# Prompt attention turned round: values stationary in two column tiles, and one product to turn the result back

## The chip, the core and the metric

The kernel runs on one core of one Trainium2 chip. The metric is the device time of one execution in microseconds (us), the median of the runs that were timed.

## The reference, cut to what matters

One layer of a hybrid encoder for a prompt of 1024 tokens and for 8 short sample sequences. The change touches one part, the attention of the prompt ("FoX", 16 heads of width 64, in float32):

```
s = (q_b . k) * 64**-0.5 + cq[q] - ck[key]     # q_b: a block of 128 queries, ck: cumulative log-forget gate
s = -inf where key > query                     # so block b sees the b + 1 key blocks up to its own
y = softmax(s) @ v                             # v: keys x 64
```

Around it stand the projection of the tokens (`z = RMSNorm(x) @ w_in`), an mLSTM over the same tokens, the attention of the samples, a merge, an expert layer (top 16 of 16384 single-neuron experts in each of 8 heads, whose rows are gathered from HBM), and a last gate. All outputs of all parts are returned.

## The kernel before

The whole layer is one program of stages with a barrier between them. Each engine has its own list of instructions, written out in order by hand, and counts semaphores to wait for the others. An engine never passes an instruction that waits, so the order of its list is part of the design.

The prompt attention stands in two stages, both built by `stage_attend`. The **small stage** takes query blocks 0 and 1 (`NB` = 2, so 32 steps of one head and one block, with 1 or 2 key blocks each; about 427 to 551 us of the span). The **large stage** takes blocks 2 to 7 (`NB` = 6, 96 steps, 3 to 8 key blocks, 5.5 in the mean; about 1855 to 2586 us). In both, the mLSTM of the same tokens rides along: 32 slots for each chunk of 128 tokens, two in each step (`ml.*_slot`, slot numbers k). In the large stage expert work rides as well (`ex.*_unit`): for each of 44 groups VectorE makes 4 dot products (L2394), ScalarE applies a Gelu to them (L2437), and VectorE weighs and adds 4 rows (L2401, L2410). There is about one Gelu in two steps, at a changing place in the step.

A step s of the attention (class `FoxPrompt`) is this chain:

1. `pe_scores` (L547, L549): TensorE makes the scores of 128 queries against up to 1024 keys in PSUM, and adds the mask. In the large stage there is one buffer for scores, so it waits until step s-1 was exponentiated.
2. `dve_max` (L581): VectorE takes the row maximum.
3. `act_exp` (L608): ScalarE makes the probabilities, and their sum.
4. `pe_turn` (L555): TensorE transposes them, a block of 128 keys at a time.
5. `act_probs` (L616): ScalarE copies the transposed blocks to `probT`.
6. `pe_mix` (L569): TensorE mixes. For each key block the 128x128 `probT` is the stationary operand and 64 columns of v are the moving one; the blocks add up in the bank `fy`.
7. `dve_y` (L588, L593): VectorE scales by the inverse sum into `y`.

The lists run this chain with an offset. TensorE's iteration s has: scores of s; transposes of the next head's q and k (`pe_head`, L531); an mLSTM slot; the turn of s-1; an mLSTM slot; the mix of s-1. ScalarE's: copies of the next head; a slot (half 0); the probability copies of s-1; the exponential of s; Gelus; a slot (half 1); Gelus. VectorE's: the maximum of s; the scaling of s-2; slots and expert units. The mix of s-1 waits for the scaling of s-2 (`y_ready`), which comes behind the maximum of s.

A float32 matmul stands in the trace as two records, each with its own weight load; a transpose is one record.

Of the kernel before, what the change touches and what calls it, by code (L numbers as in the profile page):

```python
# [17 lines left out]
ALU = mybir.AluOpType  # L18
# [3 lines left out]
P = 128  # L22
# [7 lines left out]
H_F, DF = 16, 64  # L30
# [392 lines left out]
class FoxPrompt:  # L423

    def __init__(self, nc, K, st, z, T, b0, b1):
# [9 lines left out]
        self.nmax, self.total, self.inv = (st.sb(n, [P, 2]) for n in ("fnmax", "ftotal", "finv"))  # L435
        self.y = st.sb("fy", [P, 2, NB, P])
        self.s_ps, self.y_ps = st.ps("fs", [P, 1024]), st.ps("fy", [P, 512])
        self.t_bank = [st.ps(f"ft{n}", [P, 512]) for n in range(2)]
        (self.ones_set, self.t_full, self.t_free, self.scored, self.maxed, self.expd, self.inverted, self.mixed,
         self.y_ready) = st.sems("f_ones_set f_t_full f_t_free f_scored f_maxed f_expd f_inverted f_mixed f_y_ready")  # L440
        self.qk_in, self.ck_in, self.v_in, self.y_out = (
# [93 lines left out]
    def pe_scores(self, pe, s):  # L535
        hd, b = divmod(s, self.NB)
        if s == 0:
            pe.wait_ge(self.ones_set, 1)
        if b == 0:
            pe.wait_ge(self.t_free, self.use["head", hd, len(self.groups) - 1] + 1)  # L540
            pe.wait_ge(self.ck_in[hd % 2], (hd // 2 + 1) * 16)
        if s >= self.SBUFS:
            pe.wait_ge(self.expd, s - self.SBUFS + 1)
        out, n = self.score_bank(s), self.blocks(s) * P
        for c in range(0, n, 512):
            w = min(512, n - c)
            pe.matmul(out[:, c:c + w], self.qT[:, hd % 2, b * P:(b + 1) * P], self.kT[:, hd % 2, c:c + w],  # L547
                      start=True, stop=(c + w != n))
        pe.matmul(out[:, n - P:n], self.K["ident"][:], self.K["mask"][:], start=False, stop=True).then_inc(self.scored, 1)  # L549
# [9 lines left out]
    def pe_mix(self, pe, s, r):  # L559
# [8 lines left out]
        for c in range(4 * r, min(4 * r + 4, n)):  # L568
            mm = pe.matmul(self.y_ps[:, 0:DF], self.probT[:, c * P:(c + 1) * P],  # L569
                           self.v[:, i % 2, c, e * DF:(e + 1) * DF], start=(c == 0), stop=(c == n - 1))  # L570
        if r == self.rounds(s) - 1:
            mm.then_inc(self.mixed, 1)

    def dve_first(self, dve):
        dve.memset(self.qT[DF:DF + 1, :, :], 1.0).then_inc(self.ones_set, 1)

# [7 lines left out]
    def dve_y(self, dve, s):  # L584
# [4 lines left out]
        dve.wait_ge(self.inverted, s + 1)  # L589
        dve.wait_ge(self.mixed, s + 1)  # L590
        if i >= 2:
            dve.wait_ge(self.y_out[i % 2], i // 2 * 16)
        dve.tensor_scalar(self.y[:, i % 2, b, e * DF:(e + 1) * DF], self.y_ps[:, 0:DF], self.inv[:, s % 2:s % 2 + 1],  # L593
                          None, ALU.mult).then_inc(self.y_ready, 1)
# [459 lines left out]
def stage_attend(nc, K, z, bias, cache_lf, gates, ck_last, C, m, T, b0, b1, ex=None, g0=0, g1=0):  # L1054

    with Stage(nc, f"att{b0}") as st:
# [37 lines left out]
        def _(pe):  # L1094
# [3 lines left out]
            ga.pe_scores(pe)  # L1098
            for s in range(STEPS + 1):
                if s < STEPS:  # L1100
                    fx.pe_scores(pe, s)
                    for hd, g in fx.heads_at(s):
                        fx.pe_head(pe, hd, g)
                    ml.pe_slot(pe, *slot(s, 0))
                if s >= 1:
                    for r in range(fx.rounds(s - 1)):
                        fx.pe_turn(pe, s - 1, r)
                if s < STEPS:
                    ml.pe_slot(pe, *slot(s, 1))
                if s >= 1:  # L1110
                    for r in range(fx.rounds(s - 1)):
                        fx.pe_mix(pe, s - 1, r)

        @block.scalar
        def _(act):
# [3 lines left out]
            ga.act_probs(act)  # L1119
            for s in range(STEPS + 1):  # L1120
                if s < STEPS:
                    for hd, g in fx.heads_at(s):
                        fx.act_head(act, hd, g)
                    ml.act_slot(act, *slot(s, 0))
                if s >= 1:
                    for r in range(fx.rounds(s - 1)):
                        fx.act_probs(act, s - 1, r)
# [1832 lines left out]
def trunk_kernel(nc, A, O):  # L2960
# [15 lines left out]
    with ExitStack() as ctx:  # L2976
        def sb(name, shape, dt=F32):
            return ctx.enter_context(nc.sbuf_tensor(name, shape, dt))

        K = {n: sb(n, [P, P]) for n in ("ident", "ones", "negones", "mask", "maskT", "tri", "bmask", "bmaskT", "btri",  # L2980
                                        "last", "blast")}
        K["pick"], K["inblock"] = sb("pick", [P, NSEQ]), sb("inblock", [P, NSEQ])
        K["headsel"] = sb("headsel", [H_F, 2, 8, DSEQ])
        K["masknew"] = sb("masknew", [P, DSEQ])
# [13 lines left out]
        with ExitStack() as front:  # L2998
# [4 lines left out]
            aT_later = later.enter_context(nc.sbuf_tensor("aT_later", [P, KD, (NT - FIRST) * P], F32, side="right"))  # L3003

            with nc.sbuf_tensor("aT", [P, KD, FIRST * P], F32) as aT:
                stage_front(nc, K, A["x"], A["norm_mix"], aT, aT_later, A["w_in"], z)
            stage_attend(nc, K, z, A["gate_bias"], A["cache_lf"], gates, ck_last, C, m, T, 0, FIRST - 1)
            stage_sample(nc, K, z, gates, T)
            scores_0 = front.enter_context(ExitStack())
            sc_0 = scores_0.enter_context(right("sc_0", [P, 2 * PH, PKEYS]))  # L3010
# [72 lines left out]
```

## Time and profile before

| | |
|---|---|
| median of 3 runs | 4902.13 us (4901.41 to 4904.44) |
| profiled execution | 4922.96 us |
| its span, first to last instruction | 4921.3 us |
| TensorE busy | 4366.8 us (89%) |
| VectorE busy | 3029.3 us (62%) |
| GpSimd busy | 1251.6 us (25%) |
| ScalarE busy | 960.3 us (20%) |
| mean granted TensorE clock | 0.922 of full speed |

Shares of busy time are means over stages with different limits. The two stages of the prompt attention are about 855 us of the span, and only there does the change have instructions, so they are read by themselves. The profiled execution took 20.8 us (0.4%) more than the median of the timed runs.

### The profile page before, as it was taken

The page shows a single profiled execution, that of the slowest core. Times are in us where ns is not written, and L with a number is a line of the kernel's source. Part 1 is how long each engine was busy: PE and PEld are TensorE (multiplying, and loading weights), DVE is VectorE, ACT ScalarE, POOL GpSimd, SP SyncE. Part 2 cuts the span into 40 slices and gives each one's busy share as a digit, 9 for nine tenths or more (in the row PEclk, how much of TensorE's full clock was granted, in tenths as well). Part 3 has the DMA queues.
Part 4 walks back from the last instruction along what each step waited for, and adds up shares of the span by engine and source line. Part 5 has one row for each costly group of instructions (what it writes and reads, how often), then busy time and mean ns, then how long its engine had stood idle before and what let it go on. Part 6 is the DMA issues. An engine that isn't in the chain of part 4 may idle for free. (4 is left out here: it accounts for less than half of the span.)

```text
span 4921.3 us, 48682 instructions
## 1 busy us (share of the span) xinstructions
PE 4366.8 (89%) x16974; PEld 2681.9 (54%) x16974; DVE 3029.3 (62%) x6331; ACT 960.3 (20%) x1788; POOL 1251.6 (25%) x969
## 2 busy tenths in 40 slices
PE   8996687989999978888887889768999999999988
PEld 5555453665555546666663656654545445544534
DVE  1002341457777758888881466696888777777732
ACT  1112221111111114545541111131000000000023
POOL 0000031014444432333320000003444444444400
PEclk9998788999999987778778999899999999999999
DMA  4433487759999987877858767548999999999941
GB/s 169 144 139 100 159 305 295 265 235 422 377 387 391 371 327 283 316 279 284 330 213 327 278 248 271 217 166 339 419 411 395 419 419 419 414 414 415 414 178 57
DMA packets 338726, 1477.72 MB, mean 300 GB/s; under 512 B 38146, under 2 KB 153650, under 8 KB 217938
## 3 DMA queue, kind: packets, MB, share of 16 engines
q0 software_dynamic: 119872, 824.76, 41.7%
q1 hardware_dynamic: 218642, 650.30, 35.7%
q8 instruction: 112, 1.84, 0.1%
q14 instruction: 100, 0.82, 0.0%
HBM read 1369.00 MB, written 115.38 MB: 302 GB/s over the span
## 5 line engine op out<-in xcount | busy, mean ns | idle before, releaser
L2353 POOL DMA_INDIRECT ex_uv<-in_uv,idx x768 | 1160.8, 1511 | 1902.4 <-DVE ex_acc L2410 1707.9
L2394 DVE CUSTOM_DVE_ANT_0 ex_uv<-ex_uv,ex_xp 128x1024 f32<-128x1024 f32 x768 | 912.7, 1221 | 278.5 <-DMA ex_uv<-in_uv,idx 241.7
L2410 DVE SCALAR_TENSOR_TENSOR ex_acc<-ex_uv,ex_wt,ex_acc 128x1024 f32<-128x1024 f32 x768 | 943.5, 1281 | 10.3 <-DVE C L888 3.2
L387 PE MATMUL proj_psum_acc<-proj_w,aT_later 128*128 128x385 f32 x2304 | 749.0, 487 | 9.7 <-DMA proj_w<-in_w_in 9.7
L2700 PE MATMUL exp_psum_dn<-exp_dn_big,exp_dn_gg 128*128 128x512 f32 x1536 | 686.7, 597 | 30.0 <-DVE exp_dn_gg L2622 29.9
L2691 PE MATMUL exp_psum_dn<-exp_dn_xT,exp_dn_big 128*128 128x384 f32 x2048 | 682.9, 487 | 14.8 <-DMA exp_dn_big<-in_ud 14.8
L387 PEld LDWEIGHTS proj_psum_acc<-proj_w,aT_later 128*128 128x128 f32 x2304 | 437.1, 190 | 321.1 <-DMA proj_w<-in_w_in 9.8
L2691 PEld LDWEIGHTS exp_psum_dn<-exp_dn_xT,exp_dn_big 128*128 128x128 f32 x2048 | 389.9, 190 | 314.3 <-issue 61.3
L2700 PEld LDWEIGHTS exp_psum_dn<-exp_dn_big,exp_dn_gg 128*128 128x128 f32 x1536 | 291.2, 191 | 382.0 <-issue 355.9
L296 PE MATMUL proj_psum_acc<-proj_w,aT 128*128 128x385 f32 x1152 | 377.6, 489 | 3.2 <-DVE aT L230 1.9
L2108 PE MATMUL rt_psum_b<-rt_w,rt_yT 128*128 128x512 f32 x576 | 269.0, 630 | 49.9 <-ACT rt_yT L2174 42.4
L296 PEld LDWEIGHTS proj_psum_acc<-proj_w,aT 128*128 128x128 f32 x1152 | 218.6, 190 | 158.2 <-DVE aT L230 4.0
L2141 PE MATMUL rt_psum_b<-rt_xT,rt_w 128*128 128x128 f32 x2304 | 264.4, 278 | 7.5 <-ACT rt_xT L2174 7.5
L2141 PEld LDWEIGHTS rt_psum_b<-rt_xT,rt_w 128*128 128x128 f32 x2304 | 262.9, 195 | 9.7 <-issue 9.7
L547 PE MATMUL att_psum_fs<-att_fkT,att_fqT 65*128 65x512 f32 (+3 forms) x384 | 214.2, 680 | 55.3 <-ACT att_fprob L608 32.5
L569 PE MATMUL att_psum_fy<-att_fv,att_fprobT 128*128 128x64 f32 x1152 | 185.5, 316 | 86.7 <-ACT att_fprobT L616 44.6
L1229 POOL DMA_DIRECT2D scratch_ycat<-smp_sy x128 | 61.3, 487 | 681.5 <-DVE smp_sy L1329 681.5
L569 PEld LDWEIGHTS att_psum_fy<-att_fv,att_fprobT 128*128 128x128 f32 x1152 | 168.7, 227 | 116.7 <-ACT att_fprobT L616 83.2
L2108 PEld LDWEIGHTS rt_psum_b<-rt_w,rt_yT 128*128 128x128 f32 x576 | 116.3, 204 | 197.6 <-issue 153.7
L2648 ACT ACTIVATE exp_dn_gg<-exp_psum_dn 128x384 f32<-128x384 f32 x128 | 62.6, 489 | 825.9 <-PE exp_psum_dn L2691 823.5
L2069 POOL DMA_DIRECT2D scratch_h<-rt_h x9 | 4.9, 540 | 778.3 <-DVE rt_h L2265 778.3
L2401 DVE TENSOR_TENSOR ex_wt<-ex_act,gate 128x4 f32<-128x4 f32 x192 | 30.9, 161 | 258.0 <-ACT ex_act L2437 258.0
(460 smaller groups left out, 4256.4 us busy)
## 6 DMA issues: line engine op xcount, KB each, us to landing
proj_w<-in_w_in SPq DMA_DIRECT2D x48, 1540.0 KB, 12.6
rt_w<-in_w_q SPq DMA_DIRECT2D x36, 2048.0 KB
exp_dn_big<-in_ud SPq DMA_DIRECT2D x128, 512.0 KB
exp_dn_big<-in_vd SPq DMA_DIRECT2D x128, 512.0 KB, 7.9
scratch_z<-proj_zs SPq DMA_DIRECT2D x216, 192.5 KB, 2.0
rt_w<-in_w_br_m SPq DMA_DIRECT2D x18, 2048.0 KB
rt_w<-in_w_br_f SPq DMA_DIRECT2D x18, 2048.0 KB
rt_w<-in_w_out SPq DMA_DIRECT2D x18, 2048.0 KB
```

Source lines behind the costliest of these rows:

```text
L296: mm = pe.matmul(acc[j % SLOTS][:, 0:CW], aT[:, k, t * P:(t + 1) * P], w[:, u % U, k, :], start=(k == 0), stop=(k == KD - 1))
L387: mm = pe.matmul(acc[j % SLOTS][:, 0:CW], aT[:, k, t * P:(t + 1) * P], w[:, u % U, k, :], start=(k == 0), stop=(k == KD - 1))
L547: pe.matmul(out[:, c:c + w], self.qT[:, hd % 2, b * P:(b + 1) * P], self.kT[:, hd % 2, c:c + w], start=True, stop=(c + w != n))
L569: mm = pe.matmul(self.y_ps[:, 0:DF], self.probT[:, c * P:(c + 1) * P], self.v[:, i % 2, c, e * DF:(e + 1) * DF], start=(c == 0), stop=(c = ...
L2108: mm = pe.matmul(b[:], yT[:, u * KD + k, :], ws[:, k, :], start=(k == 0), stop=(k == KD - 1))
L2141: mm = pe.matmul(b[:, c * P:(c + 1) * P], ws[:, k, c * P:(c + 1) * P], xT[:, k, :], start=(k == 0), stop=(k == KD - 1))
L2353: pool.indirect_dma_start(self.uv[:, slot, :], None, self.uv_tab, bass.IndirectOffsetOnAxis(ap=self.idx[:, at:at + 1], axis=0)).then_inc(s ...
L2394: dve.tensor_tensor_reduce(self.uv[:, slot, 0:D], self.uv[:, slot, 0:D], self.xp[:], 1.0, 0.0, ALU.mult, ALU.add, self.dot[:, g % 2, j:j + ...
L2410: dve.scalar_tensor_tensor(out=self.acc[:, j % 2, :], in0=self.uv[:, slot, D:2 * D], scalar=self.wt[:, g % 2, j:j + 1], in1=self.acc[:, j ...
L2648: act.activation(self.gg[:, c % 4, :], self.banks[3][:, c % 2 * 512:c % 2 * 512 + self.TOKENS], ACT.Gelu).then_inc(self.geluted, 1)
L2691: mm = pe.matmul(self.banks[3][:, at:at + self.TOKENS], self.big[:, q % 4, k * P:(k + 1) * P], self.xT[:, k, :], start=(k == 0), stop=(k = ...
L2700: mm = pe.matmul(self.banks[t][:, n * 512:(n + 1) * 512], self.gg[:, 4 + q % 4, t * P:(t + 1) * P], self.big[:, 4 + q % 4, n * 512:(n + 1) ...
```

## The change

The mix is turned round. For each key block, 64 columns of v become the stationary operand and the 128x128 block of `probT` the moving one. The product is the transpose of y, 64 by 128. Even key blocks write partitions 0 to 63 of the bank and odd ones partitions 64 to 127, which makes two column tiles of 64 on TensorE. ScalarE then copies this transposed pair of sums out of PSUM (`act_y`), and one more product (`pe_fold`) with a constant of two identities on top of each other adds the two halves and turns them back to 128 queries by 64. VectorE scales that.

The copy of step s-2 stands first in ScalarE's iteration s, and the new product of s-2 directly behind the scores of s on TensorE. VectorE's scaling of s-2 keeps its place, but waits for the new product instead of the mix. Five constants that only the first stages use leave the SBUF after `stage_sample`, which makes room.

```diff
@@ class FoxPrompt
+        self.yT, self.fold = st.sb("fyT", [P, 2, P]), st.sb("ffold", [P, DF])
+        self.yT_ps, self.sum_ps = self.y_ps[:, 0:P], self.y_ps[:, P:P + DF]
@@ pe_scores
         if s == 0:
-            pe.wait_ge(self.ones_set, 1)
+            pe.wait_ge(self.ones_set, 2)
@@ pe_mix
         for c in range(4 * r, min(4 * r + 4, n)):
-            mm = pe.matmul(self.y_ps[:, 0:DF], self.probT[:, c * P:(c + 1) * P],
-                           self.v[:, i % 2, c, e * DF:(e + 1) * DF], start=(c == 0), stop=(c == n - 1))
+            half = slice(c % 2 * DF, (c % 2 + 1) * DF)
+            mm = pe.matmul(self.yT_ps[half, :], self.v[:, i % 2, c, e * DF:(e + 1) * DF],
+                           self.probT[:, c * P:(c + 1) * P], start=(c < 2), stop=(c >= n - 2))
+    def halves(self, s):
+        return slice(0, DF if self.blocks(s) == 1 else P)
+
+    def act_y(self, act, s):
+        act.wait_ge(self.mixed, s + 1)
+        if s >= 2:
+            act.wait_ge(self.folded, s - 1)
+        at = self.halves(s)
+        act.copy(self.yT[at, s % 2, :], self.yT_ps[at, :]).then_inc(self.y_copied, 1)
+
+    def pe_fold(self, pe, s):
+        pe.wait_ge(self.y_copied, s + 1)
+        at = self.halves(s)
+        pe.matmul(self.sum_ps, self.yT[at, s % 2, :], self.fold[at, :], start=True, stop=True
+                  ).then_inc(self.folded, 1)
+
     def dve_first(self, dve):
+        dve.tensor_tensor(self.fold[:], self.K["ident"][:, 0:DF], self.K["ident"][:, DF:P], ALU.add
+                          ).then_inc(self.ones_set, 1)
@@ dve_y
-        dve.wait_ge(self.mixed, s + 1)
+        dve.wait_ge(self.folded, s + 1)
-        dve.tensor_scalar(self.y[:, i % 2, b, e * DF:(e + 1) * DF], self.y_ps[:, 0:DF], self.inv[:, s % 2:s % 2 + 1],
+        dve.tensor_scalar(self.y[:, i % 2, b, e * DF:(e + 1) * DF], self.sum_ps, self.inv[:, s % 2:s % 2 + 1],
                           None, ALU.mult).then_inc(self.y_ready, 1)
@@ stage_attend, TensorE
-            for s in range(STEPS + 1):
+            for s in range(STEPS + 2):
                 if s < STEPS:
                     fx.pe_scores(pe, s)
+                if s >= 2:
+                    fx.pe_fold(pe, s - 2)
+                if s < STEPS:
                     for hd, g in fx.heads_at(s):
@@ stage_attend, ScalarE
-            for s in range(STEPS + 1):
+            for s in range(STEPS + 2):
+                if s >= 2:
+                    fx.act_y(act, s - 2)
                 if s < STEPS:
                     for hd, g in fx.heads_at(s):
@@ trunk_kernel
-        K = {n: sb(n, [P, P]) for n in ("ident", "ones", "negones", "mask", "maskT", "tri", "bmask", "bmaskT", "btri",
-                                        "last", "blast")}
+        K = {n: sb(n, [P, P]) for n in ("ident", "ones", "negones", "mask", "maskT", "tri", "last")}
-        K["headsel"] = sb("headsel", [H_F, 2, 8, DSEQ])
+            sample = front.enter_context(ExitStack())
+            for n in ("bmask", "bmaskT", "btri", "blast"):
+                K[n] = sample.enter_context(right(n, [P, P]))
+            K["headsel"] = sample.enter_context(right("headsel", [H_F, 2, 8, DSEQ]))
             stage_sample(nc, K, z, gates, T)
+            sample.close()
```

## Rows read from the trace of the kernel before

**Rows 1.** Busy time by stretch: us, busy us (instructions) of each engine, clock, DMA.
```profile
427.00:551.00 124.00, 84.03 (x497) 69.76 (x495) 50.65 (x188) 48.79 (x153) 0.00 (x0) 0.87 0.26 76
1855.00:2586.00 731.00, 623.82 (x2879) 476.93 (x2877) 623.34 (x1145) 369.66 (x647) 230.88 (x168) 0.76 0.78 285
```

**Rows 2.** Waits in the large stage: who for whom, us in total, times, longest.
```profile
DVE att_fnmax L581 <- PE att_psum_fs L549: 48.6, 39, 3.7
...
DVE ex_wt L2401 <- ACT ex_act L2437: 39.4, 34, 4.0
PE att_psum_fy L569 <- DVE att_fy L593: 38.5, 25, 3.6
```

**Rows 3.** Busy time by stretch of the mix's line L569 alone (PE, PEld).
```profile
1855.00:2586.00 731.00, 167.43 (x1056) 154.72 (x1056) 0.76 0.78 285
427.00:551.00 124.00, 18.05 (x96) 13.95 (x96) 0.87 0.26 76
```

**Rows 4.** Timeline of TensorE, large stage: start, us, line, operation, records.
```profile
2198.62 1.08 PE L569 MATMUL att_psum_fy<-att_fv,att_fprobT 128*128 128x64 f32 x8 [1.57 <-DVE att_fy L593]
2199.53 2.81 PE L547 MATMUL att_psum_fs<-att_fkT,att_fqT 65*128 65x512 f32 x4
...
2229.44 3.65 PE L569 MATMUL att_psum_fy<-att_fv,att_fprobT 128*128 128x64 f32 x16
2232.88 2.02 PE L547 MATMUL att_psum_fs<-att_fkT,att_fqT 65*128 65x512 f32 x2
```

**Rows 5.** Timeline of TensorE in the stage of the samples.
```profile
602.14 1.08 PE L1289 MATMUL smp_psum_sy<-smp_svc,smp_sprobT 128*32 128x128 f32 x32
603.16 0.42 PE L1293 MATMUL smp_psum_sy<-smp_svn,smp_sprobT 16*32 16x128 f32 x8
603.51 1.13 PE L1524 MATMUL smp_psum_n<-smp_nv,smp_nkw 128*128 128x257 f32 x4
604.57 1.06 PE L1259 MATMUL smp_psum_ss<-smp_skc,smp_sqd 128*32 128x512 f32 x8
```

**Rows 6.** Timeline of TensorE in the small stage.
```profile
429.58 1.05 PE L741 MATMUL att_psum_m<-mask,ident 128*128 128x128 f32 x8
430.47 0.38 PE L555 MATMUL att_psum_ft<-ident,att_fprob 128*128 128x128 f32 x2
```

**Rows 7.** Timeline of ScalarE and TensorE in two steps of the small stage.
```profile
446.37 1.06 ACT L927 ACTIVATE att_mo<-att_mo 128x1024 f32<-128x1024 f32 x1
...
446.13 0.38 PE L531 MATMUL att_psum_ft<-ident,att_fk 128*64 128x128 f32 x2
...
501.50 0.27 ACT L616 COPY att_fprobT<-att_psum_ft 128x128 f32<-128x128 f32 x1 [1.61 <-PE att_psum_ft L555]
...
502.12 1.14 ACT L916 ACTIVATE att_mwD<-att_psum_m,att_mx 128x128 f32<-128x128 f32 x4
...
502.59 0.38 PE L531 MATMUL att_psum_ft<-ident,att_fq 128*64 128x128 f32 x2
```

**Rows 8.** Timeline of ScalarE and TensorE in one step of the large stage.
```profile
2199.17 1.28 ACT L2437 ACT_TABLE_LOAD   x1
2203.10 0.20 ACT L2437 ACTIVATE ex_act<-ex_dot 128x4 f32<-128x4 f32 x1 [2.64 <-DVE ex_dot L2394]
...
2202.56 1.06 PE L531 MATMUL att_psum_ft<-ident,att_fk 128*64 128x128 f32 x4
```

**Rows 9.** A slow stretch and the 3.4 us behind it: all instructions.
```profile
2199.60:2233.70 34.10, 33.03 (x112) 25.04 (x112) 27.56 (x47) 15.40 (x26) 9.10 (x8) 0.50 0.87 346
2233.70:2237.10 3.40, 3.40 (x14) 2.67 (x13) 1.59 (x6) 0.75 (x2) 0.00 (x0) 0.50 0.75 313
```

**Rows 10.** The same two stretches and the one behind them: line L569 alone.
```profile
2199.60:2233.70 34.10, 12.16 (x53) 11.44 (x52) 0.50 0.87 346
2233.70:2237.10 3.40, 0.00 (x0) 0.00 (x0) 0.50 0.75 313
2237.10:2257.60 20.50, 3.31 (x24) 2.90 (x24) 1.00 0.87 295
```

More of the change, by code:

```diff
@@ L436, in __init__ @@
         self.y = st.sb("fy", [P, 2, NB, P])
+        self.yT, self.fold = st.sb("fyT", [P, 2, P]), st.sb("ffold", [P, DF])
         self.s_ps, self.y_ps = st.ps("fs", [P, 1024]), st.ps("fy", [P, 512])
         self.t_bank = [st.ps(f"ft{n}", [P, 512]) for n in range(2)]
+        self.yT_ps, self.sum_ps = self.y_ps[:, 0:P], self.y_ps[:, P:P + DF]
         (self.ones_set, self.t_full, self.t_free, self.scored, self.maxed, self.expd, self.inverted, self.mixed,
-         self.y_ready) = st.sems("f_ones_set f_t_full f_t_free f_scored f_maxed f_expd f_inverted f_mixed f_y_ready")
+         self.y_ready, self.y_copied, self.folded) = st.sems(
+            "f_ones_set f_t_full f_t_free f_scored f_maxed f_expd f_inverted f_mixed f_y_ready f_y_copied f_folded")
         self.qk_in, self.ck_in, self.v_in, self.y_out = (
@@ L1104, in _ @@
                     ml.pe_slot(pe, *slot(s, 0))
-                if s >= 1:
+                if 1 <= s <= STEPS:
                     for r in range(fx.rounds(s - 1)):
@@ L1109, in _ @@
                     ml.pe_slot(pe, *slot(s, 1))
-                if s >= 1:
+                if 1 <= s <= STEPS:
                     for r in range(fx.rounds(s - 1)):
@@ L1124, in _ @@
                     ml.act_slot(act, *slot(s, 0))
-                if s >= 1:
+                if 1 <= s <= STEPS:
                     for r in range(fx.rounds(s - 1)):
```

## The prediction

> **What bounds the kernel now.** I read the page first, for the share of each engine, and then left it: the change has instructions in 855 of 4921 us only. The next view is the busy time by stretch. It shows that in the large stage TensorE and VectorE are busy for the same 624 of 731 us, with TensorE's clock at 0.76 of full speed; in the small stage nothing is busy all the time, TensorE most with 84 of 124 us [rows 1]. So in the large stage neither engine alone is the bound. They take turns, and the waits say how often. VectorE's maximum waited 39 times and 48.6 us for scores (there TensorE is late), its weights 39.4 us for ScalarE's Gelu, and TensorE's mix 38.5 us for VectorE's scaling (there VectorE is late) [rows 2]. Three steps in five are thus set by VectorE, and there a faster TensorE only waits longer. In the small stage no expert work rides along, and in the timeline TensorE's own list is the chain: mix, scores, head, slot, turn, a short wait for the copy, mix. There each instruction added to the list counts.
>
> The mix itself costs 167.4 us of TensorE in the large stage (1056 records, 528 key blocks) and 18.1 us in the small one (96 records, 48 blocks) [rows 3].
>
> **The product, before.** Start to start, 8 records took 0.91 us at full clock (114 ns each) and 16 records 3.44 us at half clock (215 ns) [rows 4]. A full-array matmul that streams 128 columns costs as much, 0.89 us for 8, or 111 ns each [rows 6]. Streaming 64 columns is thus no cheaper than 128; the weight load of 128 columns fills the time. The change loads 64 columns and streams 128, so a single tile would still take 111 ns. Only two tiles at work together make it faster.
>
> **The product, after.** No row has two tiles of 64. The nearest has four of 32: 32 records of 128 columns in 1.02 us, 32 ns each [rows 5]. A quarter of 111 would be 28, so four tiles overlap almost fully, at 1.15 times the ideal. For two tiles I take the same factor on half of 111: 64 ns at full clock, 123 at half. The bounds are 111 (no overlap) and 56 (perfect). Saved per record: 50 ns at full clock and 92 at half.
>
> The Trainium skill (TensorE: Matmul & The Clock Gate, "The mechanism") speaks against it: a weight load overlaps running matmuls only when the row group differs, and column tiles share theirs. By that each record would be load plus stream, which makes the mix slower; the 32 ns of [rows 5] disagree, being less than one stream of 128 columns.
>
> **Leaving the tiles.** Behind the tiled run, 8 records took 0.35 us where 8 times 32 ns are 0.26, and then 4 full-array records of 257 columns took 1.06 us before tiles began again, where four times 257/128 of 111 ns are 0.89 [rows 5]. A change of mode costs 0.1 to 0.2 us. Going into the tiles mostly happens behind a wait for the probability copy, which hides it. Going out, to the scores, is open: 0.15 us at full clock, 0.3 at half (bounds 0 and 0.4). The Trainium skill (TensorEngine Tiling, "Key Properties") states such a drain too, without a figure.
>
> **The new product (`pe_fold`)** is two records of 128 stationary and 64 moving columns, like the mix of one block: 0.23 us at full clock, 0.43 at half [rows 4].
>
> **Net on TensorE, a step of the large stage** (11 records): full clock 0.55 - 0.23 - 0.15 = 0.17 us saved, half clock 1.01 - 0.43 - 0.30 = 0.28 us saved. With 8 blocks it is 0.42 and 0.74 us, with 3 blocks nothing. It counts where TensorE is late, 39 steps, most of them at half clock: 39 x 0.26 = 10 us gained (bounds 0 and 18).
>
> **The small stage.** A step with one block fills one tile, so nothing is saved; with two blocks 4 x 50 = 200 ns. Against the 0.38 us of product and exit that is +0.38 and +0.18 us, 0.28 in the mean, over 32 steps 9 us lost (bounds 5 and 13: exit at nothing and at 0.3).
>
> **The copy (`act_y`)** is 128x128 elements out of PSUM, 0.27 us [rows 7]. By its length it is hidden, since ScalarE is half idle [rows 1]. Its place is the danger: it stands behind everything in ScalarE's iteration s-1, and TensorE's product of s-2 waits for it directly behind the scores of s. Queued behind that product are the next head's transposes, the slot, the turn, and behind the turn ScalarE's probability copies and the exponential that frees the score buffer. Before, TensorE waited at that place for nobody.
>
> - Small stage. The sigmoid of an mLSTM slot ended at 447.43, and TensorE had its scores done at 446.13 [rows 7]: the product would start near 447.43 + 0.27 + 0.2 = 447.9, 1.8 us later. The four exponentials of slot 7 end at 503.26, against 502.59: 1.1 us late. For the two copies of slot 3, which no row here shows, I take 1.0 us by the last one. Two chunks make 7.8 us; 7 us lost (bounds 3 and 10). In ordinary steps the copy fits beside the scores.
> - Large stage. A Gelu brings a table load of 1.28 us and 0.20 us of its own [rows 8], so the copy is done some 1.9 us after the exponential, while the scores of 3 to 8 blocks (two records of 111 ns for each block, and 0.23 us for the mask) take about 0.9 to 2.0 us at full clock and double at half. At half clock it fits; at full clock it is short by 0.5 us in the mean, 22 of 44 times. Where the last dot product is late, as in the step where TensorE was ready at 2202.56 and the Gelu came at 2203.10 [rows 8], it costs near 1.2 us in either state; I count 6 such. With the sigmoids (6 x 1 us) the sum is 11 + 7 + 6 = 24 us of TensorE's list. VectorE's lateness covers the part in steps that it sets; I charge 4 in 10: 10 us lost (bounds 3 and 24).
> - The end of each stage gets copy and product behind the last mix, about 1 us each: 2 us.
>
> **The clock.** This is the term with most play. In a slow stretch of 34.1 us TensorE was busy for 33.0 us and stayed at half clock all the same [rows 9]; 12.2 us of that was the mix (36%) [rows 10]. In the 3.4 us before the clock rose no mix ran [rows 10], and it was as busy. In the fast stretch behind it the mix is 3.3 of 17.6 us (19%) [rows 10]. So the clock is low where the mix is dense, and rose behind a stretch without it. The change halves just this part: in the slow stretch 53 x 0.123 = 6.5 us instead of 12.2, so 22%, near the fast stretch's share. I expect slow stretches to end sooner, and take 0.81 for the mean clock of the large stage: 624 x (1 - 0.76/0.81) = 38 us less busy time, of which 4 in 10 count, 15 us gained (bounds 0 for an unchanged clock and 45 for one near 0.95).
>
> **At nothing:** the constant (one addition on VectorE per stage, ahead of the first scores, which wait for a load), the moved constants (no instruction), and VectorE's changed wait (the product comes before the maximum ends, where the copy is in time).
>
> **Sum:** -10 + 9 + 7 + 10 + 2 - 15 = +3 us. Against the profiled execution that is 4923 + 3. Its time lies 20.8 us above the median of the timed runs, and I set the difference on the median, 4902.1: 4905 us. A change below 0.2% (10 us) can't be told from none here.
>
> **The rivals.**
>
> - *The terms cancel (forecast), 4893 to 4914, likeliest 4905: 0.42.* For it: each term is 7 to 15 us, and the signs are mixed.
> - *The clock comes up in earnest, 4874: 0.24.* With a clock of 0.90 the saving is 97 x 0.4 = 39 us instead of 15, and TensorE is seldom late any more. For it: [rows 9, 10]. Against it: a faster TensorE also idles more in the steps that VectorE sets, and how the clock takes that is open.
> - *The other side: the copy behind ScalarE's list, 4927: 0.21.* If the 24 us of the large stage are not covered by VectorE (+14) and the small stage loses 10 instead of 7, and the clock gives half: +3 + 14 + 3 + 8 = +28, less some overlap, 25. It decides where ScalarE's work behind the exponential outlasts the scores, from 0.9 us on with 3 blocks. For it: [rows 7, 8]. Against it: TensorE's waits for VectorE (38.5 us) are spare time.
> - *The change doesn't do what it says: the two tiles don't overlap, 4955: 0.07.* A record stays at 111 ns; product, exit and stalls come on top. Instead of -10 the large stage gets 39 x 0.6 = +23, the small one +3, and the clock gives nothing (+15): +54. Against it: [rows 5].
> - *Weight load and stream in series, 4985: 0.03.* A load of 64 columns is half of 111, so 167 ns a record, 53 more than now; 11 x 53 = 0.6 us a step at full clock and twice that at half, on 39 steps 30 us more. This is the page's rule named above.
> - The rest, 0.03, lies below 4865 or between these cases.
>
> **Range and chances.** From the clock case to the copy case with their play: 4870 to 4930; outside are the two cases without overlap and some of the tails. The likeliest case by itself spans 4893 to 4914. Faster by over 0.2% (below 4892): 0.24 and a quarter of the forecast's case, 0.33. Slower (above 4912): 0.18 + 0.10 and a sixth of the forecast's case, 0.33. Within: 0.34.
>
> **What would show it.** In the profile after, records of L569's successor should start 64 ns apart at full clock; 111 means no overlap. TensorE should wait for the copy of `yT` by name, in steps with a Gelu or the slots 3, 7 and 9: about 8 us in the small stage and 24 in the large one. The small stage should be 16 us longer. The clock of the large stage is the number to look at first: 0.81 is the forecast, 0.76 makes the kernel slower, 0.90 faster. VectorE's 48.6 us of waiting for scores should fall to some 30. What makes me wrong is most likely the clock, then the share of stalls that VectorE covers.

## The result, and the profile after

The changed kernel takes 4949.97 us in the median of 4 runs (4941.49 to 4953.97), the kernel before 4903.05 us beside it (4901.41 to 4904.44, 4 runs). The ratio is 1.0094, 95% interval 1.0076 to 1.0111: slower by 47 us (0.9%). The forecast was 4905 us in a range of 4870 to 4930, so the time lies above the range.

The first thing to look at is where the 47 us went. The profile shown of before had a large stage of 732.1 us; when the same kernel was profiled again (experiment e1), at 4897.20 us, that stage took 717.6 us at a clock of 0.78 instead of 0.76. That execution is nearer to the median, and the stages are compared with it. Busy time by stretch, first scores to first work of the next stage, and first scores to last scaling (columns as in [rows 1]); first the repeated kernel before:

```profile
419.80:551.40 131.60, 91.13 (x524) 76.19 (x524) 52.41 (x196) 53.21 (x161) 0.00 (x0) 0.85 0.30 88
1847.60:2565.20 717.60, 607.60 (x2882) 462.11 (x2882) 621.69 (x1143) 369.10 (x647) 234.57 (x168) 0.78 0.79 291
```

and the changed kernel:

```profile
418.80:572.50 153.70, 108.05 (x589) 81.60 (x589) 53.71 (x196) 61.10 (x193) 0.00 (x0) 0.83 0.26 77
1870.30:2615.00 744.70, 581.67 (x3074) 417.71 (x3074) 622.96 (x1143) 385.75 (x743) 233.22 (x168) 0.80 0.76 280
```

The small stage is 22.1 us longer and the large one 27.1 us, together the 49.4 us by which these two profiled executions differ. In the large stage TensorE has 192 records more and yet 26 us less busy time, VectorE's is the same, and the stage is longer: the loss there is waiting. In the small stage it is not waiting alone, TensorE's busy time grows by 17 of the 22 us.

The tiles do what they were meant to do. Timeline of TensorE in the large stage, 16 records at full clock and 12 at half, each up to the start of the next scores, against 114 and 215 ns a record before [rows 4]:

```profile
2200.34 1.15 PE L573 MATMUL att_psum_fy<-att_fprobT,att_fv 128*64 128x128 f32 x16 [0.24 <-ACT att_fprobT L638]
2201.41 1.13 PE L550 MATMUL att_psum_fs<-att_fkT,att_fqT 65*128 65x512 f32 x2
...
2227.42 1.55 PE L573 MATMUL att_psum_fy<-att_fprobT,att_fv 128*64 128x128 f32 x12 [0.25 <-ACT att_fprobT L638]
2228.89 1.22 PE L550 MATMUL att_psum_fs<-att_fkT,att_fqT 65*128 65x512 f32 x1
```

1.07 us / 16 = 67 ns, and 1.47 us / 12 = 122 ns, with the exit (the change from the tiles back to the full array) inside. The two tiles overlap.

The waits of the large stage (who for whom, us in total, times, longest), those of [rows 2] and two more:

```profile
PE att_psum_fs L550 <- ACT att_fprob L630: 62.7, 55, 2.2
...
DVE ex_wt L2428 <- ACT ex_act L2464: 43.6, 32, 4.3
PE att_psum_fy L591 <- ACT att_fyT L586: 40.4, 34, 2.7
DVE att_fnmax L603 <- PE att_psum_fs L552: 38.1, 40, 3.4
...
PE att_psum_fy L573 <- DVE att_fy L615: 21.0, 10, 3.4
```

TensorE now stands 34 times and 40.4 us at the new product, for ScalarE's copy. The first line is the other one that grew: TensorE waited 34.3 us for the exponential that frees the one score buffer in e1, and 62.7 us here. Its waiting for VectorE's scaling fell from 40.1 us to 21.0. One of the 34 places, ScalarE first:

```profile
2214.68 0.20 ACT L630 ACTIVATION_READ_ACCUMULATOR att_fprob<-att_psum_fs,att_fnmax 128x1 f32 x1
2214.90 1.28 ACT L2464 ACT_TABLE_LOAD   x1
2217.41 0.20 ACT L2464 ACTIVATE ex_act<-ex_dot 128x4 f32<-128x4 f32 x1 [1.23 <-DVE ex_dot L2421]
2217.53 0.25 ACT L586 COPY att_fyT<-att_psum_fy 128x128 f32<-128x128 f32 x1
...
2216.33 0.39 PE L552 MATMUL att_psum_fs<-mask,ident 128*128 128x128 f32 x2
2217.83 0.43 PE L591 MATMUL att_psum_fy<-att_ffold,att_fyT 128*128 128x64 f32 x2 [1.11 <-ACT att_fyT L586]
```

The mix had been done at about 2214.9. Its copy comes at 2217.53 only, behind a table load and a Gelu that itself waited 1.23 us for VectorE's dot product. So TensorE waits for ScalarE, which waits for VectorE, for a copy of 0.25 us whose data had been there for over 2 us.

### The profile page after: what moved, and what is told of

Read it like the earlier page. It is cut to its first block and busy times, and to the rows that moved or that the text cites. A ratio compares the mean times of both kernels' runs of the same rounds, so it can differ in the third digit from the quotient of the medians.

```text
span 4944.9 us, 49448 instructions
## 1 busy us (share of the span) xinstructions
PE 4332.7 (88%) x17230; PEld 2621.9 (53%) x17230; DVE 3030.7 (61%) x6333; ACT 984.2 (20%) x1916; POOL 1258.6 (25%) x969
## 5 line engine op out<-in xcount | busy, mean ns | idle before, releaser
L2135 PE MATMUL rt_psum_b<-rt_w,rt_yT 128*128 128x512 f32 x576 | 270.4, 633 | 50.2 <-ACT rt_yT L2201 42.4
L550 PE MATMUL att_psum_fs<-att_fkT,att_fqT 65*128 65x512 f32 (+3 forms) x384 | 199.2, 637 | 85.1 <-ACT att_fprob L630 62.7
L397 ACT COPY proj_zs<-proj_psum_acc 128x385 f32<-128x385 f32 x144 | 68.9, 480 | 627.3 <-PE proj_psum_acc L387 627.3
L573 PE MATMUL att_psum_fy<-att_fprobT,att_fv 128*64 128x128 f32 x1152 | 112.8, 314 | 72.5 <-ACT att_fprobT L638 49.9
```

Source lines behind the costliest of these rows:

```text
L573: mm = pe.matmul(self.yT_ps[half, :], self.v[:, i % 2, c, e * DF:(e + 1) * DF], self.probT[:, c * P:(c + 1) * P], start=(c < 2), stop=(c > ...
L2135: mm = pe.matmul(b[:], yT[:, u * KD + k, :], ws[:, k, :], start=(k == 0), stop=(k == KD - 1))
```

## The experiments

All runs were timed in turn with the kernel before on the same chip, whose median was 4901.23 us beside e1 to e4, 4902.72 beside e5 to e8, 4900.65 beside e9 to e12 and 4903.39 beside e13 and e14.

### e1: the kernel before, unchanged, once more

> The kernel before, unchanged, for a second profile: the first profiled execution took 4923 us, 20 us above the timed median, and the profile after took 4947, 3 us below its own. If that gap lies in the large stage (its clock differs from one execution to the next), this one shows a large stage shorter than the 732.5 us of the first profile, by up to 20 us. If it lies elsewhere, the large stage is again 732 us. Ratio to before 1.000 plus or minus 0.001.

4902.69 us (10 runs), ratio 1.0006 (0.9994 to 1.0017). Differences under some 5 us are thus within the play. The stages of its profile are shown above: the large stage is 14.5 us shorter than in the first profile, as expected. In the four other kernels with this stage unchanged (e2, e9, e10, e13) it took 714 to 725 us at a clock of 0.77 to 0.79, so the first profile's 732 us is the odd one.

### e2 and e3: the change in one stage only

```diff
+        self.tiled = b0 == 0
...
-        dve.wait_ge(self.folded, s + 1)
+        dve.wait_ge(self.folded if self.tiled else self.mixed, s + 1)
```

e3 has `b0 > 0` there. Where `tiled` is false the mix is that of before, without copy and product.

> The change in the small stage alone (blocks 0 and 1), the large stage as before. Theory A (each step of the small stage pays the product, the exit from the tiles and the waits for the copy): the small stage is 22 us longer, as in the profile after, and the kernel 18 to 22 us slower, 4921 to 4925 us. Rival (most of the loss is in the large stage, and the small stage's loss is given back in the load behind it): under 8 us slower.

> The change in the large stage alone, the small stage as before. Theory A (TensorE's 40 us of waiting for the copy fall on steps that TensorE sets, so the large stage loses 12 us and more): 4915 to 4930 us. Rival (the large stage gains by itself and the small stage loses it all): at or below 4903 us. With the small stage's run the two losses should add up to about 47 us.

e2: 4926.48 us, ratio 1.0052 (1.0036 to 1.0069). e3: 4922.23 us, ratio 1.0042 (1.0026 to 1.0059). The small stage alone costs 25 us (a little more than theory A's 18 to 22) and the large one 21; together 46, so nearly the whole 47. The small stage, 3% of the span, holds half the loss.

### e4: the copy behind the exponential

The copy of step s-1 goes directly behind the exponential of s on ScalarE's list, in place of the head of iteration s+1, so it is ahead of the Gelus and the second mLSTM slot. Nothing else changes.

```diff
-                if s >= 2:
-                    fx.act_y(act, s - 2)
...
                 if s < STEPS:
                     fx.act_exp(act, s)
+                if s >= 1:
+                    fx.act_y(act, s - 1)
```

> The change in both stages, but ScalarE's copy of the transposed result stands directly behind the exponential, ahead of the Gelu and of the slots of half 1. Theory B (the place of the copy in ScalarE's list is the main cost): TensorE's waits for the copy fall from 50 us to under 10, and the kernel to 4905 to 4925 us. Rival (the added product and the exit from the tiles are the cost): the waits fall, and the kernel stays above 4935 us.

4905.39 us, ratio 1.0011 (1.0000 to 1.0021). The waits for the copy fall to 1.6 us in the large stage and 2.6 in the small one. Moving one copy of 0.25 us gives back over 40 of the 47 us. The place of the copy is the main cause. By the profile's stages most of that is in the large one (744.7 us to 707.1); the small one keeps 15.7 of its 22.1 us (147.3 us).

### e5: the large stage alone, with the early copy

> The change in the large stage alone, with the copy of yT directly behind the exponential of the next step on ScalarE's list; the small stage mixes as before. Theory A (the tiled mix is a gain in the large stage once TensorE no longer waits for the copy): between the profiles, the large stage took 707.1 us with the early copy in both stages and 717.6 us in the repeated kernel before, so 10 us less, 4891 us (4885 to 4897). Theory B (those 10 us are the play between executions, and what the tiles save is given back by the product and the exit from the tiles): 4901 us, no difference from before.

4887.66 us, ratio 0.9968 (0.9956 to 0.9980): 15 us faster than before. The tiled mix is a gain in the large stage. Waits and busy time of the large stage, for e3 and e5, a fence for each view; first e3 (copy late):

```profile
PE att_psum_fy L596 <- ACT att_fyT L591: 45.7, 35, 2.9
...
PE att_psum_fy L575 <- DVE att_fy L620: 24.6, 11, 3.4
```

```profile
1845.90:2596.50 750.60, 577.62 (x3074) 413.94 (x3074) 622.33 (x1143) 385.96 (x743) 230.65 (x168) 0.81 0.76 278
```

e5 (copy early):

```profile
PE att_psum_fy L575 <- DVE att_fy L620: 50.2, 26, 3.7
...
PE att_psum_fy L596 <- ACT att_fyT L591: 2.4, 2, 2.0
```

```profile
1848.00:2561.10 713.10, 556.88 (x3074) 402.57 (x3074) 620.69 (x1144) 387.73 (x743) 233.88 (x168) 0.82 0.79 293
```

43.3 us of stall are gone. 25.6 of them come back as TensorE's waiting for VectorE's scaling: that is the cover that the forecast spoke of, 6 in 10, and it was right. Some 11 more come back as waits in the mLSTM slots and for the copies of the next head. But two things go the other way. The waits for ScalarE's exponential and probability copies are 10.3 us shorter in e5 (58.8 and 29.4 us, against 64.3 and 34.2), and the same 3074 records are busy for 20.7 us less. In sum TensorE is idle for 16.8 us less and busy for 20.7 us less, which is the 37.5 us by which the stage is shorter. The same product took 325 ns in the mean in e3 and 298 in e5, and from the two clocks and lengths e3's stage had about 285 us at half clock and e5's 257 (an estimate, the clocks are rounded): more of the records ran at half clock where TensorE stood. By the timed runs the stall costs 4922.2 - 4887.7 = 35 us, 8 in 10 of it.

### e6: the product behind the slot

The copy stays late; the product moves on TensorE's list, in both stages.

```diff
                     fx.pe_scores(pe, s)
-                if s >= 2:
-                    fx.pe_fold(pe, s - 2)
                 if s < STEPS:
                     for hd, g in fx.heads_at(s):
                         fx.pe_head(pe, hd, g)
                     ml.pe_slot(pe, *slot(s, 0))
+                if s >= 2:
+                    fx.pe_fold(pe, s - 2)
```

> The changed kernel in both stages with its late copy; on TensorE the new product stands behind the mLSTM slot (half 0) instead of directly behind the scores. Theory A (what costs is TensorE's list standing still behind the product that waits): the slot now covers the copy, TensorE's waits for yT fall from 50 us to under 15 us, and the time comes to 4905 to 4920 us. Theory B (what costs is that the scaling comes late, and with it the next mix): the product is later still, TensorE waits for VectorE's scaling instead, and the time stays at 4940 us or above.

4906.43 us, ratio 1.0013 (1.0004 to 1.0022). The same cure from the other side: the copy is as late as before, but work stands between the scores and the instruction that waits for it. In the large stage the waits for `yT` fall to 23.2 us, in the small one from 7.1 to 0.7 us. That is more than theory A's 15, but the time is the one that it gave. What cost most of the time was TensorE's list standing still, not the late scaling.

### e7: one column tile

e5 with `half = slice(0, DF)` for every key block, so both kinds of block use the first tile, and copy and product take 64 partitions.

> As the large-stage kernel with the early copy, but all key blocks go to the first column tile (partitions 0 to 63), so two tiles never work together; copy and product take 64 partitions. Theory A (the two tiles overlap and TensorE's time counts): records 111 ns apart at full clock instead of 67, TensorE's mix 50 to 90 us more, of which 4 in 10 count, and a product over 64 rows is 0.2 us dearer: 4915 to 4930 us. Theory B (TensorE's time hardly counts in the large stage, the waits between the engines do): within 8 us of the kernel with two tiles.

4914.69 us, ratio 1.0026 (1.0017 to 1.0035), 27 us above e5 and at the lower edge of theory A's range. Timeline of TensorE and busy time of the stage:

```profile
2197.38 1.50 PE L575 MATMUL att_psum_fy<-att_fprobT,att_fv 128*64 128x128 f32 x12 [1.04 <-ACT att_fprobT L643]
2198.81 1.98 PE L551 MATMUL att_psum_fs<-att_fkT,att_fqT 65*128 65x512 f32 x4
```

```profile
1844.20:2575.90 731.70, 606.46 (x3074) 447.01 (x3074) 620.06 (x1144) 387.94 (x743) 235.73 (x168) 0.87 0.78 285
```

1.43 us / 12 = 119 ns a record, the exit inside: one tile is no faster than the full array (114 ns), and the gain comes from the overlap of two. TensorE's 49.6 us more of busy time became 27 us of the end, 5 in 10 (the dearer product over 64 rows is part of the 49.6). Look at the clock too: a record of the mix takes as long here as before the change, and yet the stage's clock is 0.87.

### e8: no copy and no product

```diff
-                if s >= 2 and fx.tiled:
-                    fx.pe_fold(pe, s - 2)
...
-                if s >= 2 and fx.tiled:
-                    fx.act_y(act, s - 2)
```

> The large stage mixes in two column tiles, but neither the copy nor the new product is made: VectorE scales 64 columns of the transposed bank as they stand, so the prompt attention of blocks 2 to 7 is wrong in this kernel. It prices copy, product and the exit to it together. Theory A (TensorE's time counts 4 in 10): 96 products of 0.35 us and an exit of 0.15 us less, 48 us of TensorE, 19 us less than with the early copy, 4872 us. Theory B (TensorE is no longer what the steps wait for): 4888 us, as with the early copy within 5 us.

VectorE waits for the mix again and scales half of the turned bank as it stands, so this kernel leaves out what turns the result back and its outputs of the large stage are not the attention's. 4872.70 us, ratio 0.9944 (0.9929 to 0.9958), 15 us below e5. The tiles by themselves are worth 30 us, and half of that pays for turning the result back.

### e9 and e10: the small stage with the early copy; its two-block steps alone

> The change in the small stage alone, with the copy directly behind the exponential; the large stage mixes as before. Theory A (what stays once TensorE hardly waits for the copy is the price of product and exit, and it is near twice the forecast's 9 us): by the profiles the small stage takes 147.3 us so, 131.6 before, hence 4917 to 4921 us. Theory B (the forecast's 9 us was right and the rest was waiting): 4911 us.

> As the small-stage kernel with the early copy, but only the 16 steps with two key blocks use tiles, copy and product; the 16 steps with one key block mix as before. Theory A (the one-block steps are dear, since the product over 64 rows took 0.36 us where the one over 128 rows took 0.17, and they save nothing): two thirds of the loss goes, 4906 to 4909 us. Theory B (all steps pay alike, for the exit and for one more hop from engine to engine): half of it goes, 4910 to 4913 us.

e10 is e9 with `tiled(s) = self.blocks(s) == 2`, so steps with one key block mix as before. e9: 4918.75 us, ratio 1.0033 (1.0023 to 1.0042). e10: 4901.31 us, ratio 1.0001 (0.9993 to 1.0010). e9 lies where theory A had it, though only part of its reason holds, as the rows below show. In e10 theory A's direction holds, by more than it said: leaving out the one-block steps takes the whole loss away. Timeline of TensorE, mix to transposes of the next head, a one-block and a two-block step; first the repeated kernel before:

```profile
467.80 0.43 PE L569 MATMUL att_psum_fy<-att_fv,att_fprobT 128*128 128x64 f32 x2 [0.89 <-ACT att_fprobT L616]
468.07 0.44 PE L547 MATMUL att_psum_fs<-att_fkT,att_fqT 65*128 65x128 f32 x2
468.35 0.39 PE L549 MATMUL att_psum_fs<-mask,ident 128*128 128x128 f32 x2
468.57 0.38 PE L531 MATMUL att_psum_ft<-ident,att_fq 128*64 128x128 f32 x2
...
470.50 0.66 PE L569 MATMUL att_psum_fy<-att_fv,att_fprobT 128*128 128x64 f32 x4 [0.46 <-ACT att_fprobT L616]
...
471.71 0.38 PE L531 MATMUL att_psum_ft<-ident,att_fk 128*64 128x128 f32 x2
```

then e9:

```profile
467.52 0.43 PE L575 MATMUL att_psum_fy<-att_fprobT,att_fv 128*64 128x128 f32 x2 [0.89 <-ACT att_fprobT L643]
467.88 0.49 PE L551 MATMUL att_psum_fs<-att_fkT,att_fqT 65*128 65x128 f32 x2
468.21 0.39 PE L553 MATMUL att_psum_fs<-mask,ident 128*128 128x128 f32 x2
468.52 0.43 PE L596 MATMUL att_psum_fy<-att_ffold,att_fyT 64*128 64x64 f32 x2
468.89 0.41 PE L535 MATMUL att_psum_ft<-ident,att_fq 128*64 128x128 f32 x2
...
470.84 0.44 PE L575 MATMUL att_psum_fy<-att_fprobT,att_fv 128*64 128x128 f32 x4 [0.46 <-ACT att_fprobT L643]
...
471.97 0.33 PE L596 MATMUL att_psum_fy<-att_ffold,att_fyT 128*128 128x64 f32 x2
472.14 0.38 PE L535 MATMUL att_psum_ft<-ident,att_fk 128*64 128x128 f32 x2
```

A one-block step grows from 0.77 to 1.37 us, a two-block step from 1.21 to 1.30. The product over 64 rows takes 0.37 us where the one over 128 rows takes 0.17, and the mask ahead of it takes 0.31 instead of 0.22. But 16 times 0.60 and 16 times 0.09 are 11 us, and e9 lost 18. The rest goes with the clock: 0.81 over the 150.8 us of the small stage, against 0.85 over 131.6, so about 18 us more at half clock (an estimate from these four numbers). TensorE waited for the copy of a one-block step here too, 0.95 us up to 449.77, and at 449.4 there begin 10 us at half clock where the kernel before has none:

```profile
442.70:449.40 6.70, 4.52 (x29) 3.23 (x26) 3.68 (x13) 5.91 (x12) 0.00 (x0) 1.00 0.31 72
449.50:459.60 10.10, 9.20 (x29) 6.55 (x29) 2.08 (x7) 2.32 (x9) 0.00 (x0) 0.50 0.01 4
459.70:486.00 26.30, 20.78 (x126) 15.37 (x126) 13.14 (x47) 12.57 (x47) 0.00 (x0) 1.00 0.24 64
```

So e10 does not separate the two: without one-block products there is no such stall either. That took e13.

### e11: the tiles only from 5 key blocks on

> As the large-stage kernel with the early copy, but only steps with 5 or more key blocks (64 of 96) use tiles, copy and product. Theory A (at 3 and 4 blocks the tiles save what product and exit cost, as the forecast has it): within 4 us of the large-stage kernel with the early copy, 4884 to 4890 us. Theory B (the tiles gain at 3 and 4 blocks as well, because the records do not carry the whole gain): 4892 us or more.

4884.88 us, ratio 0.9971 (0.9960 to 0.9983), 3 us from e5 (1 us when each is taken against its own kernel before) and not to be told from it: at 3 and 4 blocks tiles save what product and exit cost, as theory A has it. It is the lowest time of a kernel that computes everything, 16 us below its kernel before.

### e12: early copy and later product together, large stage

> The large stage alone, with the early copy and also with the product behind the mLSTM slot (half 0) on TensorE. Theory A (with the early copy TensorE waits 2.4 us for yT in the whole stage, so there is nothing to cover, and the later scaling can only cost): 4887 to 4897 us. Theory B (the product directly behind the scores costs by its place as well): 4880 us.

4897.59 us, ratio 0.9989 (0.9980 to 0.9998), 10 us above e5 (12 when each is taken against its own kernel before), just above theory A's range. Once the copy is early nothing is left to cover, and the later product only makes the scaling, and the mix behind it, later: TensorE's mix waits 63.2 us for the scaling, against 50.2 in e5.

### e13 and e14: one stage alone, late copy, later product

> The change in the small stage alone, with its late copy, and the product behind the mLSTM slot. Theory A (product and exit cost the forecast's 9 us, and the rest of the loss is stalls behind which the clock falls to half): no stall, no fall of the clock between 442 and 480 us, 4909 to 4913 us. Theory B (each step with one key block is dearer by 1.1 us through the product itself): 4917 us or more.

> The change in the large stage alone, with its late copy, and the product behind the mLSTM slot. Theory A (the gains and losses of the stages add up): the kernel with the later product in both stages is 4 us above before and its small stage loses 9, so 5 us below before, 4894 to 4898 us; it falls short of the early copy (15 us below) because TensorE still waits 23 us for yT, and the scaling comes later. Theory B (the place of the product is as good as the place of the copy): 4888 us.

e13: 4910.61 us, ratio 1.0007 (0.9998 to 1.0016). e14: 4894.11 us, ratio 0.9984 (0.9973 to 0.9994). Theory A in both. In e13 every step has its product and none stalls: the cost is 7 us (its interval reaches from -1 to 8; by the profile the small stage is 10.2 us longer, 141.8 us), and the clock stays up in both stretches in which it fell in e9 or in the changed kernel:

```profile
441.00:478.00 37.00, 30.45 (x183) 22.62 (x183) 18.52 (x67) 20.55 (x65) 0.00 (x0) 1.00 0.22 58
494.00:540.00 46.00, 39.41 (x243) 29.96 (x243) 21.75 (x81) 24.29 (x79) 0.00 (x0) 1.00 0.12 31
```

It stays up in the repeated kernel before as well, although the mix waits there for its probability copies, for example 0.95 us:

```profile
447.94 0.43 PE L569 MATMUL att_psum_fy<-att_fv,att_fprobT 128*128 128x64 f32 x2 [0.95 <-ACT att_fprobT L616]
```

```profile
443.00:480.30 37.30, 26.71 (x163) 21.72 (x162) 18.43 (x66) 18.01 (x54) 0.00 (x0) 1.00 0.29 77
494.20:538.40 44.20, 35.27 (x223) 28.96 (x223) 22.81 (x86) 21.93 (x68) 0.00 (x0) 1.00 0.12 35
```

Against them two stalls of the changed kernel, in the timeline and by stretch:

```profile
514.55 0.39 PE L552 MATMUL att_psum_fs<-mask,ident 128*128 128x128 f32 x2
516.52 0.69 PE L591 MATMUL att_psum_fy<-att_ffold,att_fyT 128*128 128x64 f32 x2 [1.59 <-ACT att_fyT L586]
...
523.17 0.61 PE L591 MATMUL att_psum_fy<-att_ffold,att_fyT 64*128 64x64 f32 x2 [0.95 <-ACT att_fyT L586]
```

```profile
509.60:516.40 6.80, 4.07 (x30) 3.35 (x30) 2.18 (x7) 4.22 (x11) 0.00 (x0) 1.00 0.00 0
516.40:519.80 3.40, 3.27 (x10) 2.78 (x11) 0.28 (x1) 0.45 (x2) 0.00 (x0) 0.51 0.26 58
519.80:523.20 3.40, 1.51 (x9) 0.74 (x8) 2.02 (x8) 2.73 (x6) 0.00 (x0) 0.99 0.36 97
523.20:526.60 3.40, 3.29 (x10) 2.26 (x10) 1.25 (x3) 0.45 (x2) 0.00 (x0) 0.51 0.00 0
```

Here the clock falls within 0.2 us of where the product comes out of its wait. The first stall, of 1.6 us, is followed by 3.4 us at half clock, in which TensorE works nearly all the time (3.27 us).

## Why the prediction was wrong, by its own steps

**The step that failed is the price of the copy's stall** (part "The copy"): 7 us in the small stage and 10 in the large one, 17 together. Measured it is 25.3 - 7.2 = 18 us in the small stage (e2 against e13) and 35 us in the large one (e3 against e5), 53 together. (In e13 the mix waits 13.1 us for its probability copies and in e2 16.6, so some 3 of the 18 us belong to the product's new place and not to the stall.) The difference of 36 us is nearly the miss of 45. The mechanism was named, with its place on both lists, and stood as the rival "the copy behind ScalarE's list"; its price there was also too low, so even the range missed. Three things went into it.

- *Length in the large stage.* The forecast had 22 + 6 + 6 = 34 stalls of 0.7 us in the mean, 24 us. There were 34, of 1.2 us, 40.4 us (45.7 in e3). That the count agrees is luck, for its make-up differs. The forecast had 6 places with a Gelu that waits for VectorE's dot product; there were 12, with 19 of the 40 us. Most of the others stood behind a table load, a Gelu or the exponentials of a slot, up to 2.4 us long where the forecast had 0.5 and 1.0. The trace of before showed how often ScalarE waits for the dot product (large stage, ScalarE's waits):

```profile
ACT ex_act L2437 <- DVE ex_dot L2394: 28.2, 15, 3.6
```

- *The share.* Charged were 4 in 10. VectorE did cover 6 in 10 of the stall (25.6 of 43.3 us in e3 against e5), but waits for ScalarE grew by 10.3 us and TensorE's busy time by 20.7 us, so 8 in 10 came through.
- *The clock in the small stage.* The forecast's 8 us of waits were right: in the changed kernel 7.1 us before matmuls and 9.2 before weight loads. It priced them at their own length. Between 446 and 470 us and between 500 and 532 us the clock stays full in all nine profiles whose small stage is that of before, and in e6, e10 and e13. In the changed kernel, e2, e4 and e9 together it fell 8 times there, each time within 1.2 us of the end of a wait for `yT` of 0.95 to 1.59 us. There were 11 such waits, so 3 were not followed by a fall: in e4 the one that ended at 449.4 was not, the one that ended at 516.3 was. Two more waits, of 0.85 us, had no fall behind them.

  A wait's length alone does not decide it. The kernel before has eight waits of 0.89 to 0.95 us for the probability copies in these stretches, and e10 two of 1.14 us (446.67 and 508.37), all without a fall. In 6 of the 8 falls two waits stand close together, one of 0.94 to 1.14 us for the probability copies, and 2.0 us later the one for `yT`; the other 2 come with a single wait of 1.45 and 1.59 us. So the extra waits go with the falls, which is shown by the kernels that have them and by the place. It is not shown by a run that changed the clock alone, and what decides whether a wait is followed by a fall stays open.

  The Trainium skill (TensorE: Matmul & The Clock Gate, "A second HAM failure mode: psum-queue depth-cycling") tells of short idle times between groups of matmuls, often enough to make the clock go up and down, so that throughput is lost though each matmul looks fast. These rows agree in kind, with waits of 0.95 to 1.59 us; the kernel before, with eight of up to 0.95 us and no fall, shows that not every such wait does it.

**The mix in two tiles** was sized well, and a little too dear: 67 and 122 ns with the exit inside, forecast as 64 and 123 without it. With the exit of 0.09 us (below) taken out, (1.07 - 0.09) / 16 = 61 ns are left at full clock. In e7 the same working gives (1.43 - 0.09) / 12 = 112 ns for one tile, so the overlap does it.

The Trainium skill (TensorE: Matmul & The Clock Gate, "The mechanism") lets a weight load overlap running matmuls only if the row group differs. Both tiles here use all rows, and 67 ns for a weight load and a matmul, against 119 in one tile, do not fit that sentence, as the forecast had already read from the 32 ns of [rows 5].

**Product and exit** were 9 us in the small stage, measured 7 (e13), or 11 by the steps of e9, where the product stands directly behind the scores. The stage was to be 16 us longer and was 22. Inside it the steps differ from the forecast: a two-block step costs 0.09 us instead of 0.18, a one-block step 0.60 instead of 0.38. The product over 128 rows is cheaper than the 0.23 us forecast (0.17), the one over 64 rows dearer. The exit from the tiles is 0.09 us at full clock (the mix of a one-block step, 2 records, takes 0.36 us up to the scores where it took 0.27), forecast as 0.15.

**Large stage without the stall**: forecast were -10 for TensorE's net saving, -15 for the clock and about +1 for the end, -24 together. e5 measures -15. The clock came out at 0.82 where 0.81 was forecast, but the starting point was not 0.76: that profile had a long large stage, and e1 has 0.78. The forecast's reason for the rise is not borne out either. It was that the dense mix would take half the time; in e7 its records take as long as before, and the clock is 0.87. So that 0.81 was nearly met is luck, and why the clock is higher stays open. From 0.78 the forecast's own rule gives 624 x (1 - 0.78/0.81) x 0.4 = 9 us instead of 15, and the sum is -18, near the measured 15. The profiled execution was known to be 20.8 us above the median, and the forecast put that on the median without asking which stage held it; of the 25.8 us between its span and e1's, 14.5 lay in the stage whose clock carried the argument.

**The rivals.** That the clock would come up in earnest did not happen: 0.82, not 0.90, once nothing stalls. That the tiles do not overlap, or load and stream stand in series, is excluded by 67 ns. The forecast's sum of +3 with the measured terms is: large stage -15, small stage +7, stalls +53, together +45, against 47 measured. This is no further check, for the terms are taken from e2 and e3, which add up to 46 by themselves.

**Smaller slips in the forecast's sums**, which do not bear on the miss: the case in which the clock comes up in earnest is 4905 - 24 = 4881 us by its own terms, not 4874; the bounds of the small stage are 4 and 14, not 5 and 13; and the chances of faster and slower add up to 0.345 and 0.35, not 0.33.

**VectorE's waiting for scores** was to fall to 30 us; it was 38.1 in the changed kernel, and 37.4 already in e1. With the early copy (e5) it is 21.2, so TensorE did get faster where it counts, and in the changed kernel the stalls took that back.

## What to carry to other kernels

A new hop from one engine to another and back costs what stands ahead of it on the other engine's list, waits for third engines included, not what the hop itself takes. Read for each place in the loop when the copy's data are ready and when the list would come to it. Here moving 0.25 us of ScalarE's work by a few instructions was worth over 40 us, and moving the waiting product behind some other work was worth as much. Doing both in the large stage was worse than the early copy alone. The pair that the runs suggest, early copy in the large stage and later product in the small one, was not run.

Where TensorE is dense and its clock goes up and down, leave room in the price of a stall for a stretch of half clock behind it: it came with 8 of 11 here, 3.4 us and more each. And take the level of such a term (a clock, a share) from an execution near the median, or from two.

Tiling pays by size, once the copy is early: with 5 to 8 blocks the turned mix gains, with 2, 3 and 4 it is even, with 1 it loses, because one block fills one tile and brings the dearer product.

## What the runs showed of the hardware that was not expected

- Two column tiles of 64 in float32 run at 67 ns a record at full clock and 122 ns at half, the exit inside; the same records in one tile take 119 ns at full clock.
- A product with 64 rows of weights takes 0.37 us at full clock, up to the start of full-height transposes of 64 columns, where one with 128 rows takes 0.17 us; the two records ahead of it are 0.09 us longer as well. The Trainium skill (TensorEngine Tiling, "Key Properties") says that a change of tiling mode drains TensorE. If that is what the rows show, these are its prices here; no run changed the mode alone.
- With one tile (e7) TensorE had more busy time and the higher clock, 0.87 in the large stage; with two tiles it was 0.82 (e5), with the full array 0.78 (e1). These are single profiles of each kernel. Why one tile holds the clock up better stays open.
